# Moving the modulation products of a transformer front from VectorE to TensorE

## The reference

```
mod = silu(c) @ w_ada + b_ada                      # c: 1x2048, w_ada: 2048 x 6*2048
shift1, scale1, gate1, shift2, scale2, gate2 = split(mod, 6)
h = rms_norm(x, norm1_w) * (1 + scale1) + shift1
p = h @ w_in                                       # 2048 x 4112
u_f, q, k, v, o_gate, gates = split(p)
mix = concat(fourier_mix(u_f), mlstm_bidirectional(q, k, v, gates) * sigmoid(o_gate))
x = x + gate1 * (mix @ w_out)
h2 = rms_norm(x, norm2_w) * (1 + scale2) + shift2  # then the feed-forward, scaled by gate2
```

## Time and profile before

| | |
|---|---|
| time, median of 3 runs | 3658.32 us (3655.7 to 3661.67) |
| the profiled execution's own time | 3657.39 us |
| its span | 3655.5 us |
| PE busy | 3411.3 us, 93% |
| DVE busy | 2293.3 us, 63% |
| ACT busy | 1621.6 us, 44% |
| mean rate of the DMA | 195 GB/s |

### The profile page before, as it was taken

One profiled execution on the slowest core, in us unless ns is written; L12 is line 12 of the kernel. 1 busy time (PEld: TensorE's weight loads), 2 busy tenths in 40 slices (PEclk: granted clock), 3 DMA queues, 4 the chain that ended last, 5 costly groups with the idle time before them and its releaser, 6 DMA issues.

```text
span 3655.5 us, 49230 instructions
## 1 busy us (share of the span) xinstructions
PE 3411.3 (93%) x19318; PEld 2965.8 (81%) x19318; DVE 2293.3 (63%) x2473; ACT 1621.6 (44%) x1726; POOL 324.9 (9%) x411
## 2 busy tenths in 40 slices
PE   1898689999999999999999799999999899999998
PEld 1886478888888888888888699998888788888886
DVE  7876656776466564554555579996455555545555
ACT  0332245663455454543443444553343455434443
POOL 1110000000000000000000136552000000000000
PEclk9899799999999999999999899999799999999999
DMA  9997456776666666986666655667326566666664
GB/s 400 310 357 232 167 181 199 226 225 227 194 185 184 198 190 165 203 199 194 184 187 192 166 153 147 162 163 229 108 63 210 156 184 184 186 193 189 187 187 138
DMA packets 813501, 713.03 MB, mean 195 GB/s; under 512 B 13128, under 2 KB 742528, under 8 KB 805825
## 3 DMA queue, kind: packets, MB, share of 16 engines
q1 hardware_dynamic: 787840, 627.09, 58.1%
q0 software_dynamic: 20752, 79.96, 7.7%
q10 hardware_dynamic: 4784, 4.27, 0.4%
HBM read 699.47 MB, written 11.80 MB: 195 GB/s over the span
## 4 chain that ended last, share of the span: by engine, by line
PE 80%; DVE 10%; ACT 4%; issue 3%; DMA 2%; ACTq 0%; DVEq 0%
PE ps L2235 23%; PE ps L2236 12%; PE ps L2303 8%; PE ps L2307 8%; PE ps L2304 8%; DVE w_lo L1263 3%; PE ps L2254 3%; PE ps L2256 3%; PE ps L2255 3%; ACT w_hi L791 3%; PE ps L2233 2%; DMA stage<-in_w_ada 1%; DVE acc L1534 1%; PE ps L2267 1%; PE ps L2268 1%
## 5 line engine op out<-in xcount | busy, mean ns | idle before, releaser
L1263 DVE TENSOR_TENSOR w_lo<-stage,w_hi 128x2048 fp32r<-128x2048 f32 x528 | 1216.5, 2304 | 1085.3 <-ACT w_hi L791 1084.5
L791 ACT ACTIVATE w_hi<-stage 128x2048 fp32r<-128x2048 f32 x528 | 1010.6, 1914 | 1487.3 <-PE ps L2233 623.2
L2235 PE MATMUL ps<-xt,w_hi 128*128 128x512 f32 x3960 | 1419.4, 401 | 14.2 <-DVE w_lo L1263 13.0
L2236 PE MATMUL ps<-xt,w_lo 128*128 128x256 f32 x3960 | 1115.7, 282 | 0.0
L2235 PEld LDWEIGHTS ps<-xt,w_hi 128*128 128x128 f32 x3960 | 748.5, 189 | 191.5 <-DVE w_lo L1263 17.4
L2236 PEld LDWEIGHTS ps<-xt,w_lo 128*128 128x128 f32 x3960 | 752.2, 190 | 11.8
L2303 PE MATMUL ps<-w_hi,hid_hi 128*128 128x512 f32 x1152 | 449.3, 390 | 5.8 <-DVE w_lo L1263 5.8
L2304 PE MATMUL ps<-w_lo,hid_hi 128*128 128x512 f32 x1152 | 448.3, 389 | 0.0
L2254 PE MATMUL ps<-xt,w_hi 128*128 128x256 f32 x1184 | 344.0, 291 | 13.8 <-DVE w_lo L1263 9.6
L2307 PE MATMUL ps<-w_hi,hid_lo 128*128 128x512 f32 x1152 | 354.7, 389 | 0.0
L2255 PE MATMUL ps<-xt,w_hi 128*128 128x256 f32 x1184 | 336.4, 284 | 0.0
(11 more groups left out here) (406 smaller groups left out, 3794.9 us busy)
## 6 DMA issues: line engine op xcount, KB each, us to landing
stage<-in_w_in SPq DMA_DIRECT2D x92, 1024.0 KB, 5.7
stage<-in_w_up SPq DMA_DIRECT2D x88, 1024.0 KB, 5.7
stage<-in_ffn_w_gate SPq DMA_DIRECT2D x88, 1024.0 KB, 5.7
stage<-in_ffn_w_up SPq DMA_DIRECT2D x88, 1024.0 KB, 5.7
stage<-in_ffn_w_down SPq DMA_DIRECT2D x88, 1024.0 KB, 5.6
stage<-in_w_ada SPq DMA_DIRECT2D x48, 1024.0 KB, 7.4
stage<-in_w_down SPq DMA_DIRECT2D x44, 1024.0 KB, 5.1
late<-in_w_ada POOLq DMA_DIRECT2D x64, 512.0 KB, 6.5
```

What stands on the lines that cost most here:

```text
L791: act.activation(w_hi[:, u % 2 * UNIT:(u % 2 + 1) * UNIT], slot(u % SLOTS), ACT.Copy).then_inc(hi_made, 1)
L1263: dve.tensor_tensor(w_lo[:, part], slot(u % SLOTS), w_hi[:, part].bitcast(F32), ALU.subtract).then_inc(split_made, 1)
L2235: pe.matmul(dst, wh, both(k), start=k == 0, stop=False)
L2236: last = pe.matmul(dst[:, T:2 * T], wl, chunk(xt_hi, k), start=False, stop=False)
```

## The change

The 32 units of shift1 and scale1 are multiplied on PE. They are cut into column quarters: unit a covers 512 input channels and 512 outputs (a even: shift, a odd: scale), eight units a quarter, and each needs 16 matmuls with a 128x128 piece of the raw weights as the stationary operand and one column of silu(c) as the moving one, all added up in eight columns of PSUM. `zeros` opens and closes such a group of columns. The raw turned x is kept in `xraw`. After each quarter DVE forms its part of the modulation and of `xt` (`quarter_mod`). Eight row units (the first half of `in_rows`) run between and behind the quarters, then the second half, then `in_tiles`, with the gate rows and the steps of the gate chain between the tiles. The late products for gate1 and shift2 move one stage back. scale2 leaves DVE: its 16 units are multiplied on PE in the same way, six in each of the first two heads and four in the third.

```diff
-        load("ada", 16, 2, lambda i, u: [(slot(u % SLOTS), ada[u][:, i * D:(i + 1) * D])])
+            sp.dma_start(slot(at % SLOTS).rearrange("p (k n) -> p k n", k=4),
+                         ada_chunks[:, k:k + 4, cols_at:cols_at + 512]).then_inc(landed[at % SLOTS], 16)
...
+        def ada_unit(a):
+            q, at = a // 8, ada_at(a)
+            if a % 8 == 0:
+                if q >= 2:
+                    pe.wait_ge(S["mod_made"], q - 1)
+                zeros(mod_cols(q), 8, True, False)
+            pe.wait_ge(landed[at % SLOTS], 16 * (at // SLOTS + 1))
+            for x in range(4):
+                k = a % 8 // 2 * 4 + x
+                for c in range(4):
+                    w = at % SLOTS * UNIT + x * 512 + c * P
+                    last = pe.matmul(bank(MOD_BANK[q % 2], 8 * q + a % 2 * 4 + c, 1), stage[:, w:w + P], csilu[:, k:k + 1],
+                                     start=False, stop=False)
+            last.then_inc(S["ada_acc"], 1)
+            if a % 8 == 7:
+                zeros(mod_cols(q), 8, False, True).then_inc(S["mod_turned"], 1)
...
+        for a in range(8):
+            ada_unit(a)
...
+        norm(0)
+        for a in range(8, 16):
+            ada_unit(a)
+        pe.wait_ge(S["tile_copied"], 12)
+        for q in range(2, 4):
+            rows_half("in_rows", 8, 0, 0, 0, units=range(2 * q - 4, 2 * q - 2), ready=S["norm_done"])
+            for a in range(8 * q, 8 * q + 8):
+                ada_unit(a)
+        rows_half("in_rows", 8, 0, 0, 0, units=range(4, 8), ready=S["norm_done"])
+        pe.wait_ge(S["mod_made"], 4)
+        pe.wait_ge(S["cols_made"], 1)
+        rows_half("in_rows", 8, 1, 8, 8)
...
+        quarter_mod(0)
+        for q in range(1, 4):
+            quarter_mod(q)
+            split_row(2 * q - 2)
+            split_row(2 * q - 1)
+        split_row(6)
+        split_row(7)
...
+        for t in range(16):
+            split("in_tiles", 16, 0, t)
+            late(16 + 2 * t, 2)
...
-            late(66 + 4 * g, 4)
+            late(48 + 2 * g, 2)
...
-            if h < 3:
-                late(82 + 5 * h, 5 if h < 2 else 4)
+            if h < 2:
+                late(56 + 4 * h, 4)
...
+        def scale_unit(u):
+            pe.wait_ge(landed[u % SLOTS], 16 * ((plan["ada2"][0] + u) // SLOTS + 1))
+            for c in range(KC):
+                w = u % SLOTS * UNIT + c * P
+                last = pe.matmul(bank(2, c, 1), stage[:, w:w + P], csilu[:, u:u + 1], start=False, stop=False)
+            last.then_inc(S["ada_acc"], 1)
...
             if h < HEADS1 - 1:
                 scores(h + 1)
+                for u in range(6 * h, min(6 * h + 6, KC)):
+                    scale_unit(u)
```

More of the change, by code:

```diff
@@ L805, in square @@
             n = part.shape[1]
-            act.activation(turn[:, 0:n] if n <= HALF else ps[:, 2048:4096], part, ACT.Square,
+            act.activation(turn[:, 0:n] if n <= HALF else f_nat[:, 0:n], part, ACT.Square,
                            accum_out=stats[:, col:col + 1]).then_inc(S["norm_ssq"], 1)
@@ L956, in _ @@
[L956 to L963, removed]
+            elif u == 12:
+                act.wait_ge(S["wg_in"], 16)
+                act.activation(wg_hi[:, 0:KC * 16].rearrange("p (k n) -> p k n", n=16),
+                               wg_raw[:, :].rearrange("p (k n) -> p k n", n=48)[:, :, 0:16],
+                               ACT.Copy).then_inc(S["wg_split_hi"], 1)
@@ L1582, in _, with scale_second, quarter_mod @@
-        dve.wait_ge(S["csilu_made"], 1)
-        for u in range(KC):
-            ada(u)
+        def scale_second():
+            dve.wait_ge(S["mod_made"], 7)
+            link.then(dve.scalar_tensor_tensor(out=scale_cols[:, KC:2 * KC], in0=mod[:, 64:80], scalar=1.0,
+                                               in1=cols[:, C_N2:C_N2 + KC], op0=ALU.add, op1=ALU.mult))
+        def quarter_mod(q):
+            part = lambda t, at: t[:, at:at + 32].rearrange("p (v c) -> p v c", c=KC)[:, :, 4 * q:4 * q + 4]
+            dve.wait_ge(S["mod_turned"], q + 1)
+            dve.tensor_tensor(part(mod, 0), mod_cols(q).rearrange("p (v c) -> p v c", c=4),
+                              part(cols, C_ADA), ALU.add).then_inc(S["mod_made"], 1)
+            dve.wait_ge(S["mod_made"], q + 1)
+            at = slice(4 * q, 4 * q + 4)
+            link.then(dve.scalar_tensor_tensor(out=scale_cols[:, at], in0=mod[:, KC + 4 * q:KC + 4 * q + 4], scalar=1.0,
+                                               in1=cols[:, C_N1 + 4 * q:C_N1 + 4 * q + 4], op0=ALU.add, op1=ALU.mult))
+            for g in (2 * q, 2 * q + 1):
+                dve.wait_ge(S["tile_copied"], 4 + g + 1)
+                if g >= 2:
+                    dve.wait_ge(S["norm_done"], g - 1)
+                for k in range(2):
+                    c = 2 * g + k
+                    last = dve.tensor_scalar(turn[:, g % 2 * 512 + k * T:g % 2 * 512 + (k + 1) * T], chunk(xraw, c),
+                                             scale_cols[:, c:c + 1], mod[:, c:c + 1], ALU.mult, ALU.add)
+                last.then_inc(S["norm_scaled"], 1)
+            for g in (2 * q, 2 * q + 1):
+                dve.wait_ge(S["norm_hi"], g + 1)
+                rest(duo(xt_lo, g), turned_duo(g), duo(xt_hi, g), S["norm_done"])
@@ L1585, in _, with split_row @@
+        def split_row(c):
+            dve.wait_ge(hi_made, c + 1)
+            part = slice(c % 2 * UNIT, (c % 2 + 1) * UNIT)
+            dve.tensor_tensor(w_lo[:, part], slot(row_at(c) % SLOTS), w_hi[:, part].bitcast(F32),
+                              ALU.subtract).then_inc(split_made, 1)
+        dve.memset(v_one[:, :].rearrange("p (k n) -> p k n", n=257)[:, :, 256:257], 1.0)
         dve.wait_ge(S["norm_ssq"], 2)
@@ L1594, in _ @@
         dve.wait_ge(S["cols_made"], 1)
[L1595 to L1608, removed]
+        quarter_mod(0)
+        for q in range(1, 4):
+            quarter_mod(q)
+            split_row(2 * q - 2)
+            split_row(2 * q - 1)
+        split_row(6)
+        split_row(7)
+        for u in range(8, 16):
             split("in_rows", 16, 0, u)
-            late(32 + 2 * u, 2)
-            if u == 2:
-                take_mod(2, bank(7, 0, 16))
+            late(2 * u - 16, 2)
         dve.wait_ge(S["wg_split_hi"], 1)
@@ L1644, in _ @@
-        for d in range(2):
-            last = dve.tensor_tensor_scan(way(rows1, 2 + d, d), ones1[:, :], way(lfrow, d, d), 0.0,
-                                          ALU.mult, ALU.add)
-        link.then(last)
-        link.then(dve.tensor_tensor(two(rows1[:, 0:512]), igates, two(rows1[:, 512:1024]), ALU.subtract))
-        for d in range(2):
-            last = dve.tensor_tensor_scan(way(rows1, 4 + d, d), ones1[:, :], way(rows1, d, d), NEG,
-                                          ALU.mult, ALU.max)
```

374 lines of the change are left out of this document (200 added, 174 removed).

## The result

| | before | after |
|---|---|---|
| time, median of 4 runs | 3659.99 us (3655.70 to 3661.86) | 3853.3 us (3851.58 to 3854.51) |
| span of the profiled execution | 3655.5 us | 3852.7 us |
| first Fourier matmul | 314.5 us | 444.6 us |
| Fourier part, to `scores(0)` | 41.2 us | 32.1 us |
| heads, to `out1` | 72.7 us | 146.1 us |

The ratio is 1.053, with a 95% interval of 1.0511 to 1.0548. The changed kernel is 193 us slower; 3859 us were forecast, with a range of 3815 to 3890.

A forecast was written before the change was run, and what follows sets the result against it. Loads, then DVE, bound the start, PE the dense stages, engine chains the Fourier part and heads. Moving units to PE: +134.4 before the Fourier part, -8.6 in it, +75.3 in the heads, +201 us: 3859 us, range 3815 to 3890.

The forecast's parts named there:

- the price of a unit: One ada or scale unit on PE: 6.98 us at half clock, less 4 us for each stream right behind dense work.
- start of the first stream: On PE ahead of the ada units: it can start at 10.8 us, when silu(c) is there.
- four ada streams: The 32 shift1 and scale1 units on PE: 223.4 us, less 3 x 4 us for starts behind dense work, 211.4.
- three gaps: Behind quarters 1, 2 and 3 PE waits for its next row unit's split on DVE and ACT: 6.6 us each, 19.8.
- rows, tiles and what lies between: Before the Fourier part: row units 93.0 us, tiles 92.2, gate rows and transpositions 7.1, fold and half clock 5.1, waits 2.5.
- Fourier part: Gate chain, a fold and half of DVE's late products leave it: 32.6 us in place of 41.2, so -8.6 us.
- scale streams in the heads: 16 scale units on PE between scores and products: 41.9 us, then 41.9 - 4, then 27.9 - 4.
- heads: From scores to `out1`, PE alone sets the time with 16 scale units added: 148 us in place of 72.7, +75.3 us.
- Rival B: The clock comes up in the long PE streams, a unit takes 3.5 us: time 3690 us, still slower; chance 0.08.
- D: Mixed: the clock comes up in the heads' streams or for half of the time: 3775 us; chance 0.06.
- Rival C: Stationary loads overlap better, down to DVE's pace of 2.4 us a unit, so faster: 3637 us; chance 0.02.
- a sign: In the new profile, 0.50 as the granted clock in most of 11 to 270 us, with units of 7.0 us.

The follow-up runs named there:

- The versions: Two kernels with both w_ada products back on DVE, keeping the change's order of row units, tiles and gate chain; the second also mended late loads and queues: 3656.0 and 3631.3 us.
- the run with the other order: Changed kernel with the splits of a pair's two row units queued ahead of the quarter's modulation on DVE and ACT: 3829.2 us.
- the three wide matmuls: Changed kernel with 3 wide fp32 matmuls (128x128 stationary, 256 moving columns, result unused) added to each ada unit: 3931.0 us.
- the kernel with dense work in the first stream: Changed kernel with 64 moving columns in the ada units, plus 12 fp32 matmuls of 128 columns ahead of unit 3 of the first stream: 3776.6 us.

## Why the prediction was right

**The step that decided it** is the price of a unit. It was read off a fold that the kernel before already had, at the clock at which the new streams would run: 6.98 us. The streams have 6.84. Thirty-two units less 12 us for three starts at full clock were 211.4 us; the four streams sum to 208.7. Two small errors partly cancel in that: the units at the lower clock were priced 4.4 us too high, and the three starts gave back 10.4 us, not 12 (1.9, 4.0 and 4.5).

| step | forecast | measured |
|---|---|---|
| start of the first stream | 10.8 us | 8.5 |
| four ada streams | 211.4 | 208.7 |
| 38 transpositions | 7 | 7.1 |
| three gaps | 19.8 | 20.3 |
| rows, tiles and what lies between | 199.9 | about 200 |
| first Fourier matmul | 448.9 | 444.6 |
| Fourier part | 32.6 | 32.1 |
| scale streams in the heads | 103.7 | 104.1 |
| heads | 148 | 146.1 |
| all | +201 | +197.2 of span |

The transpositions are the stretch between the first two streams, 63.2 to 70.8 us, less 0.5 for `zeros`; the rows and tiles are the remainder of 444.6. The error of 4.3 us up to the Fourier part is 2.3 of the start and 2.7 of the streams, less 0.7 elsewhere. At the start, silu(c) came 2.7 us earlier (at 7.8 us; PE turns c as soon as the identity has landed, 7.5 us), which I had taken as unmoved. From the start of `out1` to the end the kernel before took 3227.1 us, the changed one 3229.9. The versions have 3227.9 and 3229.5 there, so these 2.8 us are no more than what other executions show.

**The gaps.** They were worked out as a chain of operations of DVE and ACT behind the quarter's end, and the run with the other order shows that the order of the two queues is the whole of it.

**Rival B** (the clock comes up in a long stream) is refuted by four streams of 50 to 55 us and three of 24 to 41. The heads' streams, at 5.96 to 6.83 us a unit, are much nearer to 6.84 than to 3.5, so D did not come either. It was right to give B a chance: no row of the kernel before showed a long stream, and with 64 equal columns three of the four streams did run at 1.00. By an estimate, with all 48 units at 3.59 us in place of 6.84, the change would still be slower: 3853 - 48 x 3.25 = 3697 us. Rival C's unit of 2.8 us was reached by no run that does all the work.

**What was wrong** is a sign, not a step: I expected 0.50 in the granted clock of most of 11 to 270 us. In the first 65 us the rows show 1.00 and the pace is that of 0.50 (below). And my theory after the result, that denser work would raise the clock in the streams, fell with the three wide matmuls; they made the stream 2.5 us a unit longer at 0.50.

## What to carry to other kernels

Before work moves to the matrix engine, find the same instruction in the trace and take its time in a stretch like the one it will stand in: a stream of one-column matmuls kept PE 100% busy at 1.2 GHz, and a unit that DVE did in 2.40 us took 6.84. An idle engine does not take work for nothing when the work lies on the chain that sets the end; ask what the busier engine will hold up, here every head. When a change bundles a costly part with a cheap reordering, run the reordering alone: it held 7 us in the Fourier part, and its own new waits had eaten most of them until the queues were put in the order in which they are waited for.

## What the hardware showed that I had not expected

**The granted clock's column can read 1.00 where the pace is that of 1.2 GHz.** Two windows of the kernel with dense work in the first stream:

```profile
11.00:33.00 22.00, 22.00 (x105) 22.00 (x105) 2.04 (x3) 7.49 (x7) 4.58 (x7) 1.00 0.93 305
33.00:38.00 5.00, 5.00 (x42) 5.00 (x42) 0.00 (x0) 0.00 (x0) 0.00 (x0) 1.00 0.42 162
```

Both read 1.00, with 0.21 and 0.12 us a record. The same is seen in the changed kernel: 1.00 in all windows up to 72 us, at 0.21 us a record until the transpositions, and the first lower reading at the first fall (0.97 in 72 to 73 us, 0.50 behind it). Up to there the time of one record tells the clock and the column does not.

**A stream held a clock that it had not raised.** 64 columns a matmul: 20.58 us at 6.86 us a unit before the dense work, 17.98 us at 3.60 behind it.

**Up to 64 moving columns were free at the lower clock.** 64 in place of one changed the first stream's time by 0.03 us, where PE's weight loads are busy all the time (40.00 of 40.00 us in the first window of the changed kernel). 512 were not: the two records of the first `zeros` took 2.07 us in place of 0.60 with 8.
